# A decoder layer on one core: output projection and second layer norm drawn into the attention stage

## The reference

```python
x = layer_norm(ALPHA * x + 0.5 * swiglu_1(x))     # first FFN, inner width 2816
m = concat([retention_group(x), sliding_window_attention(x)]) @ w_out   # 512 + 512 columns
x = layer_norm(ALPHA * x + m)                     # second layer norm
x = layer_norm(ALPHA * x + 0.5 * swiglu_2(x))     # second FFN
```

## Time and profile before

| | |
|---|---|
| time before, median of 3 runs | 2187.69 us (2186.79 to 2191.33) |
| the profiled execution, its own time | 2191.25 us |
| its span, first to last instruction | 2189.1 us |
| TensorE busy | 2116.2 us (97% of the span), 11989 matmuls |
| VectorE, ScalarE, GpSimd busy | 911.7, 506.9, 518.3 us |
| mean granted TensorE clock | 0.982 of full speed |

### The profile page before, as it was taken

How to read it: one execution, slowest core, us unless ns; L and a number is a source line. 1 busy time by engine, 2 the same in 40 slices (tenths; PEclk the granted TensorE clock), 3 DMA queues, 4 the chain that set the end, 5 groups by cost and what they waited for, 6 DMA issues and landing times. The chain is left out here.

```text
span 2189.1 us, 31133 instructions
## 1 busy us (share of the span) xinstructions
PE 2116.2 (97%) x11989; PEld 1941.3 (89%) x11989; DVE 911.7 (42%) x1690; ACT 506.9 (23%) x887; POOL 518.3 (24%) x257
## 2 busy tenths in 40 slices
PE   8999999999999989999996899899999999999997
PEld 8999999999999979998794478899999999999996
DVE  5535343434434361003535724343434353535346
ACT  4121112111111251211235723211111112111215
POOL 3221212121221241222242412322121212121213
PEclk9999999999999999999898999999999999999999
DMA  7011110101010121111112030101010111101012
GB/s 281 31 56 50 36 57 29 57 29 57 29 57 30 39 101 39 39 38 42 61 65 99 1 120 1 58 30 58 29 57 29 57 35 52 51 35 57 29 58 82
DMA packets 38058, 118.40 MB, mean 54 GB/s; under 512 B 6255, under 2 KB 10863, under 8 KB 37743
## 3 DMA queue, kind: packets, MB, share of 16 engines
q1 hardware_dynamic: 37999, 117.58, 15.1%
HBM read 106.29 MB, written 11.27 MB: 54 GB/s over the span
## 5 line engine op out<-in xcount | busy, mean ns | idle before, releaser
L113 PE MATMUL bank<-x_hi,f_w_hi 128*128 128x362 f32 (+1 forms) x2104 | 688.8, 327 | 6.5 <-issue 5.6
L115 PE MATMUL bank<-x_hi,f_w_low 128*128 128x362 f32 (+1 forms) x2104 | 690.5, 328 | 0.0
L357 POOL TENSOR_TENSOR f_w_low<-f_w_raw,f_w_hi 128x1024 fp32r<-128x1024 f32 x132 | 317.3, 2419 | 1179.9 <-ACT f_w_hi L287 1179.9
L545 DVE TENSOR_TENSOR acc<-bank,acc 128x512 f32<-128x512 f32 x720 | 467.1, 688 | 8.2 <-PE bank L443 5.8
L523 DVE TENSOR_TENSOR f_h_full<-bank,f_silu 128x362 f32<-128x362 f32 (+1 forms) x132 | 70.7, 535 | 818.6 <-PE bank L115 816.3
L113 PEld LDWEIGHTS bank<-x_hi,f_w_hi 128*128 128x128 f32 x2104 | 396.9, 189 | 8.7 <-issue 6.9
L115 PEld LDWEIGHTS bank<-x_hi,f_w_low 128*128 128x128 f32 x2104 | 396.4, 188 | 0.0
L114 PE MATMUL bank<-x_lo,f_w_hi 128*128 128x362 f32 (+1 forms) x1056 | 345.9, 328 | 0.0
L114 PE MATMUL bank<-x_low,f_w_hi 128*128 128x362 f32 (+1 forms) x1048 | 342.9, 327 | 0.0
L441 PE MATMUL bank<-f_w_hi,f_h_hi 128*128 128x512 f32 x640 | 250.8, 392 | 0.0
L443 PE MATMUL bank<-f_w_low,f_h_hi 128*128 128x512 f32 x640 | 250.2, 391 | 0.0
(11 more groups left out here) (196 smaller groups left out, 2243.2 us busy)
## 6 DMA issues: line engine op xcount, KB each, us to landing
f_w_raw<-ffn_in SPq DMA_DIRECT2D x132, 512.0 KB, 4.4
rp_w_raw<-w_ret_in SPq DMA_DIRECT2D x16, 512.0 KB, 3.5
acc<-x_rows_in SPq DMA_DIRECT2D x2, 2048.0 KB, 11.1
kept_rows<-acc SPq DMA_DIRECT2D x8, 512.0 KB, 2.9
ow_raw<-w_out_in SPq DMA_DIRECT2D x8, 512.0 KB, 6.9
y_out<-acc SPq DMA_DIRECT2D x8, 512.0 KB, 2.7
n_rows<-ln_rows_in SPq DMA_DIRECT2D x6, 512.0 KB, 8.5
acc<-kept_rows SPq DMA_DIRECT2D x2, 1536.0 KB, 9.7
```

Source lines behind the costliest of these rows:

```text
L113: pe.matmul(out, wh, xh, start=first, stop=False)
L115: return pe.matmul(out, wl, xh, start=False, stop=last)
L357: pool.tensor_tensor(flat(w_lo[s][j]), flat(w_raw[s][j]), flat(w_hi[s][j]).bitcast(F32), ALU.subtract).then_inc(done, 1)
L545: dve.tensor_tensor(acc[:, t, d], down_ps[(n + 2 * s) % 4][:, :], acc[:, t, d], ALU.add).then_inc(down_free, 1)
```

## The change

The output projection and the second layer norm move into the attention stage (`attention_and_projection_stage`), so that attention's block is also that of the projection and of the second FFN.

- The projection's 18 halves are now called units, 24 passes each. Iteration i of attention (from 6 on, `LAG`) ends with unit i - 6, which belongs to the token tile three behind. So twelve units (`BETWEEN`) stand inside attention, all in bank 7, each waiting until VectorE has added the one before; the last six follow, in banks 2 to 5, each with a turn behind it.
- Attention's outputs of both heads share bank 6, on different partitions.
- VectorE adds unit i - 7 at the end of its iteration i. From iteration 18 on it also finishes normed tiles (`gained_tile`), and it packs the sample tile after iteration 19.
- The out weights are rounded and split in the first six iterations, two of them twice.
- ScalarE's `deviation` of tile p stands in iteration 14 + p; after attention it alternates with `high`. GpSimd's gains of tiles 0 to 5 follow its last item, then come the FFN's first two splits, then the gains of tiles 6 and 7.
- SyncE loads token rows 0 to 3 right behind the out weights and the others, the gain row and the bias row when their room comes free, each behind a wait. `load_bias` also waits for the first gain.
- The tiles are taken in plain order, samples last (`order`); the sample tile's last norm step is on 64 partitions. Some tensors move (caches, `q_rows`, the norm's statistics). The semaphore `topped` is folded into `maxed`.
- The second FFN's first step takes three turns instead of two, with the roundings and low parts that belong to them, in a new order on ScalarE.

```diff
 class Norm:
+    def load_gain(self, sp, src):
+        sp.dma_start(self.rows[:, 0, :], src[0]).then_inc(self.rows_loaded, 16)
+
+    def load_bias(self, sp, src):
+        sp.wait_ge(self.gained, 1)
+        sp.dma_start(self.rows[:, 1, :], src[1]).then_inc(self.rows_loaded, 16)
+
...
 # FFN, ScalarE
+        def first_step_with_norm():
+            silu_chunk(0, 0, 0)
+            first_norm.high(act, TOKEN_TILES - 3)
+            round_h(0, 0, 0)
+            first_norm.high(act, TOKEN_TILES - 2)
+            round_part(act, 1, 1, GATE)
+            silu_chunk(0, 0, 1)
+            first_norm.high(act, TOKEN_TILES - 1)
+            round_h(0, 0, 1)
+            round_part(act, 1, 1, UP)
+            round_part(act, 0, 0, DOWN)
+            silu_and_round(0, 0, 2)
...
 # FFN, TensorE
         else:
-            gate_up(0, 0, 0)
-        if first_norm:
+            gate_up(0, 0, 0, between=lambda: first_norm.turn(pe, TOKEN_TILES - 3))
             first_norm.turn(pe, TOKEN_TILES - 2)
             pe.wait_ge(*banks_free)
             gate_up(0, 0, 1, between=lambda: first_norm.turn(pe, TOKEN_TILES - 1))
...
+    UNITS, LAG = 2 * TOKEN_TILES, 6
+    BETWEEN = LAST - LAG
+    ROUNDED_AT = {0: (0,), 1: (1,), 2: (2, 3), 3: (4, 5), 4: (6,), 5: (7,)}
+    ROWS_OF = {0: 0, 1: 0, 2: 0, 3: 0, 4: 1, 5: 1, 6: 2, 7: 3, 8: 4}
...
-    score_ps, turn_ps, out_ps = [core.banks[0:2], core.banks[2:4]], core.banks[4:6], core.banks[6:8]
+    score_ps, turn_ps, out_ps = [core.banks[0:2], core.banks[2:4]], core.banks[4:6], core.banks[6]
+    unit_ps = core.banks[2:6]
...
     def sync(sp):
         for k in range(KT):
             out_weights.load(sp, k)
+        for done in kept_done:
+            sp.wait_ge(*done)
+        load_rows(sp, 0, 0, 4)
...
         sp.wait_ge(stored, 16 * (5 + DEC_BATCH))
+        sp.wait_ge(scored, LAST)
+        norm.load_gain(sp, ln_rows)
+        load_rows(sp, 2, 6, 7)
+        sp.wait_ge(biased, LAST - 2)
+        load_rows(sp, 1, 4, 6)
+        sp.wait_ge(out_done, LAST - 2)
+        norm.load_bias(sp, ln_rows)
+        sp.wait_ge(out_done, LAST)
+        load_rows(sp, 3, 7, 8)
+        sp.dma_start(acc[0:DEC, BLOCKS, :], kept[BLOCKS, 0:DEC, :]).then_inc(rows_in[4], 16)
...
+        def unit(n):
+            t, d = n // 2, slice(512 * (n % 2), 512 * (n % 2) + 512)
+            if n < BETWEEN:
+                out = core.banks[7]
+                if n:
+                    pe.wait_ge(proj_free, n)
+                if n % 2 == 0:
+                    pe.wait_ge(lo_done, KVH * (t + 1))
+            else:
+                out = unit_ps[n % 4]
+                if n == BETWEEN:
+                    pe.wait_ge(biased, LAST)
+                if n >= BETWEEN + 4:
+                    pe.wait_ge(proj_free, n - 3)
+                if t < BLOCKS:
+                    pe.wait_ge(lo_done, KVH * (t + 1))
+                else:
+                    pe.wait_ge(packed, 3)
+            for k in range(KT):
...
+                if n == 0:
+                    pe.wait_ge(out_weights.lo_done, k + 1)
+                pe.matmul(out, high, out_weights.hi[k][:, d], start=k == 0, stop=False)
+                pe.matmul(out, low, out_weights.hi[k][:, d], start=False, stop=False)
+                mm = pe.matmul(out, high, out_weights.low[k][:, d], start=False, stop=k == KT - 1)
+            mm.then_inc(proj_done, 1)
...
             if i:
                 output(i - 1)
+            if 0 <= i - LAG < BETWEEN:
+                unit(i - LAG)
+        for n in range(BETWEEN, UNITS):
+            unit(n)
+            if n == BETWEEN:
+                pe.wait_ge(lo_done, LAST)
+                pe.wait_ge(proj_free, BETWEEN)
+            norm.turn(pe, n - BETWEEN)
...
+        def add_unit(n):
...
+            dve.wait_ge(proj_done, n + 1)
+            dve.scalar_tensor_tensor(acc[r, t, d], acc[r, t, d], ALPHA, ps[r, :],
+                                     ALU.mult, ALU.add, accum_out=norm.row_sum(t, half)).then_inc(proj_free, 1)
+            if half:
+                norm.mean(dve, t, (proj_free, n + 1))
+
+        def gained_tile(p):
+            norm.invert(dve, p)
+            norm.shift(dve, p)
...
             if i >= 2:
                 low_part(i - 2)
-            if 1 <= i <= KT:
-                out_weights.split(dve, i - 1)
+            for k in ROUNDED_AT.get(i - 1, ()):
+                out_weights.split(dve, k)
+            if 0 <= i - LAG - 1 < BETWEEN:
+                add_unit(i - LAG - 1)
+            if i >= LAST:
+                gained_tile(i - LAST)
...
+        for n in range(BETWEEN, UNITS):
+            if n > BETWEEN:
+                norm.low(dve, n - BETWEEN - 1)
+            gained_tile(n - BETWEEN + 2)
+            add_unit(n)
+        norm.low(dve, UNITS - BETWEEN - 1)
+        norm.centre_and_gain(dve)
+        gained_tile(TOKEN_TILES - 1)
...
+            for k in ROUNDED_AT.get(i, ()):
+                out_weights.round(act, k)
+            if i >= LAST - SLOTS:
+                norm.deviation(act, i - LAST + SLOTS)
+        norm.deviation(act, 5)
+        norm.high(act, 0)
...
-def output_projection_stage(core, weights, mix_hi, mix_lo, pack, acc, kept, kept_done, norm):
...
-    one_stage_block(nc, attention)
```

More of the change, by code:

```diff
@@ L652, in tile @@
     def tile(self, p):
-        return self.acc[self.part(p), ORDER[p], :]
+        return self.acc[self.part(p), self.order[p], :]
     def part(self, p):
-        return slice(0, DEC) if ORDER[p] == BLOCKS else slice(0, P)
+        return slice(0, DEC) if self.order[p] == BLOCKS else slice(0, P)
     def load_rows(self, sp, src):
@@ L702, in shift @@
         r = self.part(p)
+        if self.apart and p == 0:
+            dve.wait_ge(self.rows_loaded, 32)
         dve.wait_ge(self.inverted, p + 1)
@@ L746, in keep @@
         sp.wait_ge(self.affine, p + 1)
-        sp.dma_start(self.kept_at[ORDER[p], self.part(p), :], self.tile(p)).then_inc(self.kept(p)[0], 16)
+        sp.dma_start(self.kept_at[self.order[p], self.part(p), :], self.tile(p)).then_inc(self.kept(p)[0], 16)
     def kept(self, p):
@@ L1742, in low_part @@
                 dve.tensor_tensor(mix_lo[d, PAIRS:2 * PAIRS, P * n:P * n + P],
-                                  out_ps[h][d, :].rearrange("p (t q) -> p t q", t=GROUP),
+                                  out_ps[d, :].rearrange("p (t q) -> p t q", t=GROUP),
                                   mix_hi[d, PAIRS:2 * PAIRS, P * n:P * n + P].bitcast(F32),
                                   ALU.subtract).then_inc(lo_done, 1)
+        def add_unit(n):
+            t, half = n // 2, n % 2
+            r, d = norm.part(t), slice(512 * half, 512 * half + 512)
+            ps = core.banks[7] if n < BETWEEN else unit_ps[n % 4]
+            if half == 0 and (t == 0 or ROWS_OF[t] != ROWS_OF[t - 1]):
+                dve.wait_ge(rows_in[ROWS_OF[t]], 16)
+            dve.wait_ge(proj_done, n + 1)
[6 more added lines that the diff above has]
+            norm.shift(dve, p)
         for i in range(-SLOTS, LAST + 2):
@@ L1912, with gpsimd_second @@
+        for p in range(6):
+            norm.gain(pool, p)
+    def gpsimd_second(pool):
+        norm.gain(pool, 6)
+        norm.gain(pool, 7)
+    return Stage(sync_early=sync_early, sync=sync, tensor=tensor, vector=vector, scalar=scalar, gpsimd=gpsimd,
+                 scalar_second=scalar_second, gpsimd_second=gpsimd_second,
+                 products_done=(proj_done, UNITS), added=(proj_free, UNITS))
 SMALL = {}
@@ L1927, in decoder_layer_kernel @@
         decoder_layer(core, i, o)
-def one_stage_block(nc, stage):
-    with nc.Block() as block:
-        block.sync(stage.sync)
-        block.tensor(stage.tensor)
-        block.vector(stage.vector)
-        block.scalar(stage.scalar)
-        block.gpsimd(stage.gpsimd)
 def decoder_layer(core, i, o):
@@ L2109, in decoder_layer @@
     ffn2 = ffn_stage(core, "f2_", ffn2_buffers, i["ffn2"], part("fold"), acc, xh2, xl2, wait_x2, norm2.acc_ready, norm3,
-                     room=out_proj.products_done, banks_free=out_proj.added, first_norm=norm2)
+                     room=attention.products_done, banks_free=attention.added, first_norm=norm2)
     with nc.Block() as block:
@@ L2146, in _ @@
         def _(pe):
-            out_proj.tensor(pe)
+            attention.tensor(pe)
             ffn2.tensor(pe)
```

191 lines of the change are left out of this document (72 added, 119 removed).

## The result

| | before | after |
|---|---|---|
| time, median of 11 runs | 2187.44 us (2185.13 to 2192.53) | 2194.71 us (2191.34 to 2198.05) |
| the profiled execution, its own time | 2191.25 us | 2197.65 us |
| its span | 2189.1 us | 2195.8 us |
| mean granted TensorE clock | 0.982 | 0.982 |

The ratio is 1.0031, with a 95% interval of 1.0021 to 1.0040: 7.3 us slower, where 0.1 us less was forecast.

What follows compares the result with a forecast made beforehand. The sum of TensorE's matmul passes bounds most of the kernel. From item 6's transposes to the FFN's first two products, 176.7 us plus 6.2 for clock made 182.9 against 183.0 before, so 2187.6 us, range 2180 to 2195.5.

Steps and rivals of the forecast that it cites:

- The wait on bank 7: Units 1 to 7 in attention: TensorE waits until VectorE has added the unit before, 18.0 us in all.
- The clock: Units behind the five waits of 2.9 us: four start at half clock, 1.55 us each, 6.2 us in all.
- clean sums: Attention iterations without clock loss: 11.44 us each for 7, 9 and 11, 13.29 each for 8 and 10.
- Iteration 6: First attention iteration with a unit: no bank to wait for, 1.00 + 1.92 + 1.87 + 5.6 = 10.4 us.
- its last weight: Unit 0 needs the eighth weight split for its last three passes: 0 to 2.2 us, taken as 1.0.
- Units 12 to 17: Last six units, behind attention: four banks and a turn each, no wait, 6 x (5.6 + 0.87) = 38.8 us.
- The rival of GpSimd holding VectorE up: From unit 11 on, GpSimd's gains and splits slow VectorE's norm work: 6 us more, 2193.6 us, chance 0.17.
- Ahead of item 6: Attention before item 6's transposes: two more weight splits on VectorE, between 0 and 2.4 us, taken as 1.2.
- The FFN's start: Second FFN's first two products with one turn: the 5.64 us gap and the half clock go, 9.2 us in all.
- every wait loses the clock: Rival for the units in attention: half clock costs 13.1 us, 6.8 us over 183.0, 2194.5 us, chance 0.11.

Runs made afterwards that it cites:

- e1: The changed kernel with VectorE's addition of unit i - 7 moved from the end to the head of its iteration: 2171.44 us, ratio 0.9923 to the kernel before.
- e6: The changed kernel with ten unread passes (five before units 6 and 7) ahead of units 1 to 7 on TensorE: 2191.11 us, ratio 1.0012 to the kernel before.
- e2: The changed kernel with ScalarE's rounding `high(1)` put ahead of `deviation(6)`: 2189.61 us, ratio 1.0012 to the kernel before.
- e4: The changed kernel with GpSimd's first two splits for the second FFN put behind the gain of tile 6: 2191.76 us, ratio 1.0021 to the kernel before.
- e7: The kernel before with its out weights rounded and split in the order of the changed kernel: 2187.82 us, ratio 1.0000 to the unedited kernel before.
- e5: The changed kernel with two clearings of a 128 x 1024 tile ahead of VectorE's addition of units 0 to 5: 2212.93 us, ratio 1.0118 to the kernel before.

## Why the prediction was wrong

The mechanism of the units' waits held, but the rest of the sum was too small, and the forecast came out on the wrong side of zero: by the traces 7.6 us were missing. The largest miss is the step from unit 12 on, which had no wait in it. Step by step:

- *The wait on bank 7* was right in place, cause and size: 2.97 and 2.90 us forecast, 3.08 and 2.74 measured; 1.6 and 1.7 against 1.31 and 1.66; 18.0 in all against 17.7. e1 shows the cause: the additions' place in the queue. None before units 8 to 17, as said.
- *The clock*: four of five such waits lost it, as taken, in units 1, 3, 4 and 5. A lost one cost more than 1.55: iterations 7, 9, 10 and 11 are 1.8, 1.8, 1.5 and 1.8 over their clean sums, 6.9. e6 bears out the size.
- *Iteration 6* was mis-sized by the prediction's own row. It was put at 10.4 us with a score pair of 1.92; the earlier trace rows show that very pair at 3.35, at half clock behind the wait of 2.26, in the kernel before. It is 3.40 after, and the iteration 12.13. Against this, unit 0 did not wait for its last weight (1.0 forecast, 0 measured). The iterations together: 135.7 against 133.7.
- *Units 12 to 17* failed most: "Units 12 to 17 have four banks and a turn each: 6 x (5.6 + 0.87) = 38.8", measured 43.2. Of the 4.4, 2.58 is turn 2's wait and 1.57 the half clock behind it, as e2 shows. The rival of GpSimd holding VectorE up had the overlap right but asked for it "in most tiles". It took two hits (e4 takes the second away), because ScalarE's queue made tile 1's rounding wait for tile 6's mean. That order was in the diff's functions and was not walked through; only VectorE's load was added up.
- *Ahead of item 6*: 2.55 us in this pair of traces, not 1.2, and just above the upper bound of 2.4. The forecast priced the splits' own time only. They lengthen item 4's wait by 0.95 us, and the longer wait lost the clock, 1.6 us, a term that the sum did not have there. The kernel before gets the time back behind item 6 when its splits are made early (e7); in the kernel after nothing does, as its iterations were costed without a split already. How much of this an average execution pays is not known: seven other executions of the same code took 1.8 to 2.0 us less ahead of item 6.
- *The FFN's start* was right: no gap and no half clock, 9.1 us against 9.2.

The errors are +1.35 ahead of item 6, +2.0 in the iterations, +4.4 behind them and -0.1 at the FFN: 7.6. The forecast set 24 us of waits and clock lost against as much gained from holes and barriers. It was a difference of two large sums, so these few terms decided its sign. Of the other rivals, that every wait loses the clock is not what happened (unit 2 kept it), though its 2194.5 is the time that came; the agreement is by other terms.

The Trainium skill, "TensorE: Matmul & The Clock Gate", section "HAM oscillation — how this bites in real kernels", describes a kernel whose short bursts of matmuls lie between DMA waits longer than the bursts, and where every burst starts at half clock. Here the waits are shorter than the units of 5.6 us, and the traces agree only in part: half clock followed four of the seven in the kernel after, and all six of 3.5 to 5.5 us in e5.

Open: why 2.74 us kept the clock before unit 2 and lost it before unit 4. It is not a chance of one execution, as the traces of e2 and e4 have the same five waits with the same outcome in each. No run here was made to tell the reason.

## What to carry to other kernels

Put the operation that frees a single buffer at the head of the freeing engine's iteration: the same instruction at the other end of the iteration was worth 23 us here, since what stood before it waited for the engine that wanted the buffer. When work of two stages is drawn together, walk each engine's queue for an instruction that waits on a later tile ahead of one that an earlier tile needs, ScalarE's too, and not the engines' loads alone. Price a wait of some 3 us between dense stretches at its length plus what the half clock behind it costs, 1.5 to 1.8 us here in four of five, and read that first in the rows of the kernel before. Compare a stretch in more than one execution before a difference of 2 us in it is put down to an edit: the same code took 48.4 or 50.4 us here.

## What the hardware showed beyond that

- Some forms suffer beside GpSimd and others don't. CAST 128x512 from 0.42 to 2.64 us and SCALAR_TENSOR_TENSOR 128x1024 from 1.28 to 3.23, both with all their tiles in SBUF; the addition (0.69) and the low part (1.22), which read a bank, ran at their own length beside GpSimd's splits at 1354.15.
- Two CASTs of the same form, one after the other, took 0.42 and 2.64 us: the first began 0.06 us ahead of GpSimd's gain (1348.45 and 1348.51), the second behind it.
- Passes that nobody reads, in a wait that stays, gave 6.2 us back: each unit still began 5.97 us after its transposes (1223.11 to 1229.08 in e6, 1221.75 to 1227.72 after), but at full clock.
